# Recurrence: v centred as it is turned over, roots written for 64 channels and transposed, the bonus as two half products, the second head's E made from M

## What is computed

```python
    kk = heads(k * k_k).astype(jnp.float32)
    kk = kk / jnp.maximum(jnp.sqrt(jnp.sum(kk * kk, axis=-1, keepdims=True)), 1e-12)
    ...
    y = rwkv7_scan(rh, heads(decay), kh, vh, kk, ah)
    mean = jnp.mean(y, axis=-1, keepdims=True)
    var = jnp.mean(jnp.square(y - mean), axis=-1, keepdims=True)
    y = (y - mean) * lax.rsqrt(var + GN_EPS)
    y = y * lnx_w... + lnx_b...
    bonus = jnp.sum((rh * kh * r_k), axis=-1, keepdims=True) * vh
    y = (y + bonus)
    return y * g
```

```python
        sa = jnp.einsum('bhij,bhj->bhi', S, -kk_t)
        S = (S * w_t[:, :, None, :] + sa[..., None] * (kk_t * a_t)[:, :, None, :]
             + v_t[..., None] * k_t[:, :, None, :])
        y = jnp.einsum('bhij,bhj->bhi', S, r_t)
```

## Time and profile before

| | |
|---|---|
| Time, median of 3 runs | 2340.56 us (2339.53 to 2345.85) |
| The profiled execution's own time | 2338.43 us |
| Its span in the profile | 2336.7 us |
| TensorE busy | 2290.9 us, 98% of the span |
| DVE, ACT, POOL busy | 1157.2, 913.7, 1161.4 us |
| Mean granted TensorE clock | 0.994 of full speed |
| Pairs 0 to 3 of the recurrence | from about 1144.8 to 1352 us |

### The profile page before, as it was taken

The page is one execution under the profiler, slowest core; times in us unless marked ns, Lnnn a source line. Parts: engine busy times, 40 slices in busy tenths (PEclk is TensorE's granted clock), DMA queues, the critical chain, the costliest instruction groups (busy, mean ns, idle before and its releaser), DMA issues.

```text
span 2336.7 us, 37010 instructions
## 1 busy us (share of the span) xinstructions
PE 2290.9 (98%) x13984; PEld 1892.6 (81%) x13984; DVE 1157.2 (50%) x1773; ACT 913.7 (39%) x1456; POOL 1161.4 (50%) x687
## 2 busy tenths in 40 slices
PE   8999999999999999999999989999999999999998
PEld 7888887888888888877777777888888877888887
DVE  5442146267743331377544466714625986731732
ACT  5332225467753321255644263212234435321222
POOL 5444444545565554444555343444445973544442
PEclk9999999999999999999999999999999999999999
DMA  4332233310033233232111112233222332332321
GB/s 166 99 98 92 97 99 108 119 62 1 2 108 99 90 99 99 95 121 64 46 40 46 47 55 87 94 98 99 93 96 83 99 100 82 99 99 90 98 95 58
DMA packets 56127, 200.11 MB, mean 86 GB/s; under 512 B 6224, under 2 KB 6480, under 8 KB 56016
## 3 DMA queue, kind: packets, MB, share of 16 engines
q1 hardware_dynamic: 54432, 195.82, 25.9%
q10 hardware_dynamic: 1584, 2.75, 0.4%
HBM read 196.45 MB, written 2.10 MB: 85 GB/s over the span
## 4 chain that ended last, share of the span: by engine, by line
PE 44%; POOL 4%; issue 3%; DVE 2%; ACT 1%; POOLq 0%; DVEq 0%; ACTq 0%
PE ps L133 13%; PE ps L135 13%; PE ps L134 12%; POOL sb_w_lo L114 2%; POOL sb_caway L3031 1%; PE ps L641 1%; PE ps L2044 0%; DVE ps L3082 0%; PE ps L656 0%; POOL sb_cout L3037 0%; POOL sb_cu_lo L3043 0%; PE ps L2040 0%; PE ps L2091 0%; PE ps L2020 0%; PE ps L1989 0%
## 5 line engine op out<-in xcount | busy, mean ns | idle before, releaser
L114 POOL TENSOR_TENSOR sb_w_lo<-sb_w_raw,sb_w_hi 128x1024 fp32r<-128x1024 f32 (+1 forms) x361 | 884.6, 2453 | 943.3 <-ACT sb_w_hi L101 941.9
L133 PE MATMUL ps<-sb_xn_hi,sb_w_hi 128*128 128x512 f32 x1688 | 669.6, 397 | 4.9 <-POOL sb_w_lo L114 2.8
L134 PE MATMUL ps<-sb_xn_lo,sb_w_hi 128*128 128x512 f32 x1688 | 658.0, 390 | 0.0
L135 PE MATMUL ps<-sb_xn_hi,sb_w_lo 128*128 128x512 f32 x1688 | 658.0, 390 | 0.0
L101 ACT ACTIVATE sb_w_hi<-sb_w_raw 128x1024 fp32r<-128x1024 f32 x362 | 379.8, 1055 | 480.3 <-PE ps L135 454.2
L133 PEld LDWEIGHTS ps<-sb_xn_hi,sb_w_hi 128*128 128x128 f32 x1688 | 316.4, 187 | 76.7 <-issue 4.0
L135 PEld LDWEIGHTS ps<-sb_xn_hi,sb_w_lo 128*128 128x128 f32 x1688 | 316.6, 188 | 67.7
L134 PEld LDWEIGHTS ps<-sb_xn_lo,sb_w_hi 128*128 128x128 f32 x1688 | 316.8, 188 | 65.7 <-issue 2.2
L133 PE MATMUL ps<-sb_hid_hi,sb_w_hi 128*128 128x512 f32 x864 | 336.3, 389 | 2.0 <-DVE sb_hid_lo L401 2.0
L134 PE MATMUL ps<-sb_hid_lo,sb_w_hi 128*128 128x512 f32 x864 | 336.1, 389 | 0.0
L135 PE MATMUL ps<-sb_hid_hi,sb_w_lo 128*128 128x512 f32 x864 | 336.1, 389 | 0.0
(11 more groups left out here) (487 smaller groups left out, 2998.6 us busy)
## 6 DMA issues: line engine op xcount, KB each, us to landing
sb_w_raw<-weights SPq DMA_DIRECT2D x365, 512.0 KB, 3.4
sb_stage<-x SPq DMA_DIRECT2D x4, 512.0 KB, 4.9
out<-sb_out_stage SPq DMA_DIRECT2D x8, 256.0 KB, 2.8
sb_abias<-table ACTq DMA_DIRECT2D x4, 256.0 KB, 5.0
sb_lora_w<-lora ACTq DMA_DIRECT2D x2, 256.0 KB, 2.7
sb_rstd<-table ACTq DMA_DIRECT2D x1, 256.0 KB, 2.8
sb_root<-table ACTq DMA_DIRECT2D x1, 256.0 KB, 3.1
sb_ss<-table ACTq DMA_DIRECT2D x1, 256.0 KB, 4.9
```

The lines of the kernel that those rows point to most:

```text
L114: pool.tensor_tensor(c.w_lo[:, slot, 0:width], c.w_raw[:, slot, 0:width], c.w_hi[:, slot, 0:width].bitcast(F32), ALU.subtract).then_inc(c. ...
L133: pe.matmul(out, hi, rhs_hi(k0 + k), start=first, stop=False)
L134: pe.matmul(out, hi, rhs_lo(k0 + k), start=False, stop=False)
L135: mm = pe.matmul(out, lo, rhs_hi(k0 + k), start=False, stop=last)
```

## The change

It has four parts and what they need.

1. **V is centred as it is turned.** In place of a transpose with the identity, V's four blocks are multiplied with `centre`, the identity less 1/64 in each head's block. The products then carry v less its mean over the head's channels, and so y comes out with mean zero. `mean` and `yc` go; `ysq` squares y itself and stands ahead of the turned tiles on ACT.
2. **Roots for 64 channels, transposed.** DVE first forms `kmax` and the reciprocal `rec` of the summed squares (at level 1 instead of 2), ACT then takes the root with each value read 64 times, 128x512 values, and PE transposes four blocks in place of the eight matmuls. The tail's `yadd`, `yrec`, `yroot`, `yrb` go the same way, and the tail's `var` moves from behind level 1 to behind level 0.
3. **The bonus as two half products.** ACT makes the high part `rkh` of its operand, POOL the low part `rkl`, and PE two fp32r matmuls that accumulate.
4. **The second head's E from M.** DVE multiplies the two halves of M's block with the mask into E, with the halves of the partitions exchanged (two operations of 64 partitions). The eight matmuls on L1999 go.

Three small operations on POOL make `centre` and `ones_part` among the constants, in the first block's stage.

**POOL in the second preparation (beside pair 0), before:** the low weight parts follow on the two subtractions that need L (`lp`, `le`).

The diff, cut to its core:

```diff
 def rwkv_preparation():
     pe = ["lora_w", "lora_a", "kknorm", "kkb", "bonus"]
-    act = ["k1", ..., "root", "sigw", "siga", "ld", "rks", "eP", "ePi", "ePp", "ePn", "ePe"]
-    dve = ["raw1", "raw0", "raw2", "rootmax", "rec", "L", "kk", "bon"]
+    act = ["k1", ..., "root", "sigw", "siga", "ld", "rks", "eP", "ePi", "rkh", "ePp", "ePn", "ePe"]
+    dve = ["raw1", "raw0", "raw2", "kmax", "rec", "L", "kk", "bon"]
...
+def spread(norm):
+    return norm[:, 1].rearrange("p b s -> p (b s)").unsqueeze(2).broadcast_to([P, 2 * TT, HD])
...
 rwkv_pe, prepare:
         elif part == "kkb":
-            PV(j, "rec")
+            PA(j, "root")
             if j >= 2:
-                TA(j - 2, "yroot")
-            mm = by_channel_pe(pe, c, b_norm, w.norm)
+                TV(j - 2, "yrec")
+            for b in range(TT):
+                mm = pe.transpose(ps[:, b_norm, b * P:b * P + P], w.tmp2[:, b * P:b * P + P], c.ident[:])
         else:
-            PL(j, "rk")
             PV(j, "kk")
-            mm = pe.matmul(ps[:, bonus_bank(u, j)], c.ones_head[:], w.rk, start=True, stop=True)
+            bank = ps[:, bonus_bank(u, j)]
+            PA(j, "rkh")
+            pe.matmul(bank, c.ones_part, w.rk_hi[:], start=True, stop=False)
+            PL(j, "rkl")
+            mm = pe.matmul(bank, c.ones_part, w.rk_lo[:], start=False, stop=True)
...
 rwkv_pe, tail:
-        if name == "mean":
-            if t < PAIRS - 1:
+        if name == "var":
+            if t == PAIRS - 2:
                 pe.wait_ge(c.s_evac, first_unit(t + 2) + START + 3)
-            mm = pe.matmul(ps[:, bank], c.ones_head[:], w.YL[:], start=True, stop=True)
-        elif name == "var":
-            if t < PAIRS - 2:
-                PA(t + 2, "root")
             TA(t, "ysq")
...
-            TV(t, "yrec")
-            mm = by_channel_pe(pe, c, bank, w.ynorm)
+            TA(t, "yroot")
+            for b in range(TT):
+                mm = pe.transpose(ps[:, bank, b * P:b * P + P], w.ysq[:, b], c.ident[:])
...
 rwkv_pe, steps of a pair:
         done("prod", mm)
-        tail(t, "mean")
...
-        for b, p in ((b, p) for b in range(TT) for p in range(2)):
-            mm = pe.matmul(ps[across(1, p), 5, ...], w.BK[HALF[1], 2 * b + p, 0],
-                           AR[HALF[1], 0, token(b, p)], start=True, stop=True)
         done("lab", mm)
...
+                if name == "V":
+                    mm = pe.matmul(turned, w.v[:, b * P:b * P + P], c.centre, start=True, stop=True)
+                else:
+                    mm = pe.transpose(turned, sources[x][:, b * P:b * P + P], c.ident[:])
...
-            if lv == 1:
+            if lv == 0:
                 tail(t, "var")
...
 rwkv_act:
         elif part == "root":
-            PE_(j, "kknorm")
-            prepared("root", act.activation(w.norm[:, 0], ps[:, b_norm, 0:2 * TT]..., ACT.Sqrt))
+            PV(j, "rec")
+            prepared("root", act.activation(w.tmp2.rearrange("p (x n) -> p x n", n=HD), spread(w.norm), ACT.Sqrt))
...
             prepared("ePi", act.activation(w.ePi, w.L[:], ACT.Exp, scale=-1.0))
+            PL(j, "rk")
+            if j >= 1:
+                PE_(j - 1, "bonus")
+            prepared("rkh", act.activation(w.rk_hi[:], w.rk, ACT.Copy))
...
         if name == "ysq":
-            TV(t, "yc")
-            ended("ysq", act.activation(w.ysq, w.yc, ACT.Square))
+            V(t, "y")
+            ended("ysq", act.activation(w.RU[:], w.YL[:], ACT.Square))
         else:
-            TE(t, "var")
+            TV(t, "yrec")
...
+        tail(j - 1, "ysq")
         for name, x, bank in TURNS:
...
 rwkv_pool:
         prepared("le", ...)
+        PA(j, "rkh")
+        prepared("rkl", pool.tensor_tensor(w.rk_lo[:], w.rk, w.rk_hi[:].bitcast(F32), ALU.subtract))
         if j >= 1:
             stream_low(pool, c, base + 6 + 3 * j, base + 9 + 3 * j)
...
 rwkv_dve:
         elif part == "rec":
-            PA(j, "root")
-            prepared("rootmax", dve.tensor_scalar(w.norm[:, 0], w.norm[:, 0], 1e-12, None, ALU.max))
+            PE_(j, "kknorm")
+            prepared("kmax", dve.tensor_scalar(w.norm[:, 0], sums, 1e-24, None, ALU.max))
...
-        if name == "yc":
-            ...
-        elif name == "yrec":
-            TA(t, "yroot")
+        if name == "yrec":
+            TE(t, "var")
+            ended("yadd", dve.tensor_scalar(w.ynorm[:, 0], sums, 1.0 / HD, GN_EPS, ALU.mult, ALU.add))
...
-        done("em1", dve.tensor_tensor(w.E[:, 1], ps[:, 5, TT * CH:]..., first, ALU.mult))
+        dve.tensor_tensor(w.E[HALF[1], 1], w.M[HALF[0], 1, :, 0], first[HALF[0]], ALU.mult)
+        done("em1", dve.tensor_tensor(w.E[HALF[0], 1], w.M[HALF[1], 1, :, 0], first[HALF[1]], ALU.mult))
...
-            elif lv == 2:
+            elif lv == 1:
                 prepare(q, "rec")
+                tail(t, "yrec")
```

More of the change, by code:

```diff
@@ L1622, in rwkv_tail @@
 def rwkv_tail():
-    return ["mean", "var", "yrb", "gate"], ["ysq", "yroot"], ["yc", "yrec", "yn", "ysum", "out"]
+    return ["var", "yrb", "gate"], ["ysq", "yroot"], ["yadd", "yrec", "yn", "ysum", "out"]
 PREPARATION = dict(zip(("pe", "act", "dve", "pool"), rwkv_preparation()))
@@ L2116, in rwkv_pe @@
     scores(0)
-    V(t, "y")
-    tail(t, "mean")
     out_early(4, 6)
@@ L2679, in rwkv_dve @@
     add_early(0)
-    tail(t, "yc")
     maxima(0)
```

50 lines of the change are left out of this document (22 added, 28 removed).

## The result

| | before | after |
|---|---|---|
| Time, median of 20 runs each, on the same chips | 2340.18 us | 2346.14 us (2344.57 to 2348.35) |
| Ratio | 1 | 1.0025, 95% interval 1.0018 to 1.0032 |
| Span of the profiled execution | 2336.7 us | 2345.0 us |
| Mean granted TensorE clock in it | 0.994 | 0.987 |
| First products of pairs 0, 1, 2, 3 start at | 1144.8, 1193.4, 1245.9, 1299.2 | 1145.6, 1199.5, 1254.7, 1308.7 |

The changed kernel is slower by 0.25%, less than the 0.3% set as the border, and 1.1 us above the predicted 2345.

What follows compares the result with a forecast made beforehand. TensorE, at work 98% of the span, was taken to bound it. Terms 3.1 + 0.5 − 1.46 − 1.3 = +0.9, clock +4.5, sum +5.4 us: 2343.8 on the profile, 2346.0 against the median; forecast 2345, range 2334 to 2351.

Steps and rivals of the forecast that it cites:

- the wait at the eighth fill: PE, opening a new weight unit, waits 3 to 4 us for POOL's low weight part in pairs 0 to 2.
- pair 3: Last pair of the recurrence, which prepares nothing and has no wait for a low weight part: −1.46 us.
- the stage behind the pairs: Last pair's mean and spread, lying among output products and attention: −1.45 us, of which −1.3 was taken.
- PE's work: Matmul work dropped or added on TensorE: −2.53 us per pair, −10.1 in all, the most the change could give.
- both vanish: On PE: the mean's 0.86 us and the 0.56 us of matmuls for the second head's E go entirely.
- The gate's chain, pair 1: POOL's rkl directly ahead of the low weight parts, waiting for ACT's rkh: the low part starts 1.2 us later.
- Pair 0: First pair: PE's first products 0.2 us later, ACT's table load 2.0, low weight part 3.1; in all +3.1 us.
- No longer by L: Chain to the low weight part runs by ACT's root, load, exps, rkh and rkl, not DVE's L; no size.
- The clock: Behind three longer waits for the low part, TensorE falls to half clock: 1.5 us each, +4.5, bounds 0 and 5.1.
- Clock holds: Rival: waits for the low part don't lower TensorE's clock, only +0.9 us remains: 2339.3, or 2341.5 against the median; chance 0.20.
- The saving arrives: Rival: rkl doesn't delay POOL's low weight part, all −10.1 us shows: 2328.3 to 2330.5; chance 0.10.
- rkl at its dear price: Rival: POOL's rkl takes 2.14 us beside DVE work, not 1.27: in all +8.9, 2347.3 to 2349.5; chance 0.18.

Runs made afterwards that it cites:

- low_first: The changed kernel with the first of POOL's three low weight parts moved ahead of lp: 2330.84 us, ratio 0.9951 to the kernel before.
- warm_gate: The changed kernel with 12 extra matmuls of unused result on PE just ahead of the eighth fill in pairs 0 to 2: 2341.23 us.

## Why the prediction came out right

**The total** was 1.1 us off by the medians; the profiled executions lie 8.3 apart, where the sum had 5.4. The main steps hold: the wait at the eighth fill grew in pairs 0 to 2, the chain leaves by ACT and rkl in pairs 1 and 2, the low clock stands at the gates, pair 3 is shorter by 1.36 (1.46 predicted), the stage behind the pairs by 1.54 (1.3). But several terms had the wrong size, and that they cancelled is luck.

**PE's work.** PE reaches the eighth fill of pair 1 26.05 us after the pair's first products, before 28.25: 2.20 us less, where the prediction had 1.46. Mean 0.84 (0.86), spread 0.61 (0.59). V's turn cost 0.46 (0.55), with 0.18 at the turn of B and K beside it, and the second head's E brought 0.46 (0.56). Two gains were not in the sum at all. The product `lora_a` used to wait for `yc` from the second pair on; with `yc` that wait went, the two half-height products run side by side (as they did in pair 0 before, where the wait did not stand), and 0.49 is saved. And `var` waits no longer for ACT's root and takes 0.43 less. The step that failed here is "both vanish": I counted the operations that go and not the waits that go with them. Behind the gate it was the other way round: the bonus gave 0.33, not 0.48, and with the tail's spread 0.50 in all (low_first), not 1.07.

**The gate's chain, pair 1.** Predicted +1.2, measured +0.71 (30.07 after the first products, before 29.36). The load did not stay where it was but moved 0.52 earlier, since PE's gains ahead of it are larger than I had. Price and place of rkl were right: 1.26 (1.27), directly ahead of the low part, waiting for rkh. With 2.20 for PE the gap is 1.11 + 2.20 + 0.71 = 4.02, as measured; 3.8 was predicted.

**Pair 0.** Predicted +2.9 beyond its start, measured +2.93 in the second profile of the changed kernel, where no stretch of this pair was slow. But the way there was another, and the match is luck. The load came 2.6 us later relative to the first products (I had 2.0 in all, 1.8 beyond the start), and yet the exps were not what delayed the low part. It is the sum of DVE's scan starting 1.23 later, the scan taking 2.27 in place of 1.21, because the later load had put POOL's rk right beside it, and rkl's 1.24: 3.5 us. "No longer by L" is thus wrong for this pair, and its low part is later by 3.5, not 2.9; behind the gate 0.6 came back that I had put at nothing. Nor did PE come to this gate as I had it. It came 27.65 us after the first products, before 26.20, so 1.45 later, with less work: on the way it waited 1.00, 0.45 and 0.75 us for DVE (M, D and D again), before only 0.46. So the gap was 2.7 and not 3.5. The first of these waits:

```profile
1150.95 0.69 PE L1990 MATMUL ps<-sb_BK,sb_AR 64*64 64x64 f32 x32 [1.00 <-DVE sb_M L2606]
```

The start came 1.0 later against the norm's product, not 0.2; there POOL's two subtractions behind rk took 1.75 and 2.02 beside DVE work, before 1.31 and 1.50.

**The clock.** Predicted 1.5 a gap, +4.5. Measured: 2.4 in pair 0 (its length of 53.90 in this profile against 51.48 in the second, whose clock stayed up), 2.6 and 2.3 in pairs 1 and 2, where the low clock began within the wait and still held for 5.3 and 4.6 us behind it, and 1.6 behind the 1.93 us wait of the next stage, where the kernel before had no fall. Together this is 8.9 in this profile, and the largest error of the prediction: I had taken the length of a slow stretch from one row of before, and a wait of 4 us brings one twice as long. It does not show in the total, because without the clock the sum is −0.8 instead of +0.9 (start +0.8, pair 0 +2.9, pair 1 0.0, pair 2 −1.6, pair 3 −1.4, behind −1.5; of pair 2's 1.6, 0.75 is the idle stretch that its state step had before, where the prediction took pair 2 for pair 1 over again), and because the profiled execution of before was one at 0.994, while over 43 of its runs the clock was 0.992 on the mean; over 20 of the changed kernel it was 0.988.

**The rivals.** "Clock holds" is what warm_gate made of the kernel by force: 2341.23, predicted 2341.5. "The saving arrives" is low_first: 2330.84, predicted 2328.3 to 2330.5. "rkl at its dear price" did not happen, 1.27, 1.26 and 1.27 in three pairs; but the same dear price fell on rk in pairs 1 and 2, 2.08, and there it was on the chain, as `lp` waits for it. Before the change rk was done early.

## What to carry to other kernels

When PE is busy 98% of the time, look for the operation that feeds it on an in-order engine, and count what every edit puts ahead of that operation: here the first of three low weight parts needed nothing of what stood before it, and moving it by hand was worth 15 us of the changed kernel, more than all the saved matmuls. In the kernel before, whose gates waited 1.1 us and less, the same move gave nothing clear of noise. Of an operation that goes, list the waits that go with it; of a guard that is kept, ask what stands before it in its new place. Before DVE or POOL work is moved, see what the other engine does at that minute: an operation that is off the chain can stop one that is on it.
